# Turning the injection round in an S5 mixer: tokens as the standing operand, states in token order, two modulation panels moved to later joins

## The reference

```python
def s5_scan(u, lam_bar, b_bar, h0, reverse):
    bu = jnp.einsum('bngc,gsc->bngs', u.astype(jnp.complex64), b_bar)
    a = jnp.broadcast_to(lam_bar, bu.shape)
    a_cum, xs = lax.associative_scan(_lin_rec, (a, bu), axis=1, reverse=reverse)
    return xs if h0 is None else xs + a_cum * h0[:, None]
...
        xs_ctx = s5_scan(u_ctx, lam_bar, b_bar, None, reverse)
        h0 = xs_ctx[:, 0] if reverse else xs_ctx[:, -1]
        xs_lat = s5_scan(u_lat, lam_bar, b_bar, h0, reverse)
        y_lat = y_lat + jnp.einsum('bngs,gcs->bngc', xs_lat, c_mat).real.reshape(B, L, D)
```

## Time and profile before

| | |
|---|---|
| median of three timed runs | 2246.18 us (2245.98 to 2246.7) |
| the profiled execution: its time, its span | 2244.69 us, 2242.9 us |
| busy in the span: PE, DVE, ACT, POOL | 2102.9, 1164.0, 865.2, 158.9 us |
| mean granted clock of PE | 0.958 of 2.4 GHz |
| the chain that ended last, by engine | PE 88%, DVE 6%, DMA 3%, ACT 2% |

### The profile page before, as it was taken

One profiled execution on the slowest core, in us unless ns is written; L12 is line 12 of the kernel. 1 busy time (PEld: TensorE's weight loads), 2 busy tenths in 40 slices (PEclk: granted clock), 3 DMA queues, 4 the chain that ended last, 5 costly groups with the idle time before them and its releaser, 6 DMA issues.

```text
span 2242.9 us, 31627 instructions
## 1 busy us (share of the span) xinstructions
PE 2102.9 (94%) x13233; PEld 1648.8 (74%) x13233; DVE 1164.0 (52%) x1961; ACT 865.2 (39%) x1416; POOL 158.9 (7%) x225
## 2 busy tenths in 40 slices
PE   4999999999999989988999999997959899898998
PEld 2756566777787767754558888875948799778997
DVE  2322562656566567636154665765571645526454
ACT  2442233443333453220244334245632544525444
POOL 0000110102001100010001200111120000000000
PEclk8999999999999999999999999998579999999999
DMA  6334442545445546531143433444584555314553
GB/s 256 132 116 175 135 148 68 168 154 182 155 153 175 173 154 224 186 134 65 38 151 118 130 118 115 134 134 166 207 336 135 188 188 188 125 57 150 188 178 105
DMA packets 227243, 342.14 MB, mean 153 GB/s; under 512 B 9590, under 2 KB 190625, under 8 KB 224860
## 3 DMA queue, kind: packets, MB, share of 16 engines
q1 hardware_dynamic: 216064, 310.27, 40.4%
q0 software_dynamic: 10320, 29.58, 4.5%
q10 hardware_dynamic: 716, 0.26, 0.0%
HBM read 317.66 MB, written 24.51 MB: 153 GB/s over the span
## 4 chain that ended last, share of the span: by engine, by line
PE 88%; DVE 6%; DMA 3%; ACT 2%; issue 1%; SPq 0%; ACTq 0%; DVEq 0%
PE bank L956 21%; PE bank L957 20%; PE bank L958 20%; PE bank L819 4%; PE bank L397 4%; PE bank L864 2%; PE bank L2473 2%; DMA mod_ring<-mod_w 2%; PE bank L1722 1%; PE bank L1351 1%; PE bank L637 1%; DMA arena<-mod_w 1%; PE bank L2055 1%; PE bank L627 1%; PE bank L1676 1%; PE bank L1933 1%
## 5 line engine op out<-in xcount | busy, mean ns | idle before, releaser
L956 PE MATMUL bank<-h_hi,w_hi 128*128 128x512 f32 (+1 forms) x1480 | 512.4, 346 | 10.9 <-DVE h_lo L725 10.3
L957 PE MATMUL bank<-h_lo,w_hi 128*128 128x512 f32 (+1 forms) x1480 | 504.9, 341 | 0.0
L958 PE MATMUL bank<-h_hi,w_lo 128*128 128x512 f32 (+1 forms) x1480 | 504.8, 341 | 0.0
L917 DVE TENSOR_TENSOR w_lo<-ring,w_hi 128x1024 fp32r<-128x1024 f32 (+1 forms) x282 | 323.9, 1186 | 285.6 <-ACT w_hi L910 285.5
L956 PEld LDWEIGHTS bank<-h_hi,w_hi 128*128 128x128 f32 x1480 | 283.2, 191 | 49.2 <-DVE h_lo L725 12.3
L910 ACT ACTIVATE w_hi<-ring 128x1024 fp32r<-128x1024 f32 (+1 forms) x282 | 274.0, 1019 | 104.7 <-PE bank L958 103.1
L958 PEld LDWEIGHTS bank<-h_hi,w_lo 128*128 128x128 f32 x1480 | 283.1, 191 | 32.2 <-issue 0.2
L957 PEld LDWEIGHTS bank<-h_lo,w_hi 128*128 128x128 f32 x1480 | 283.6, 192 | 29.5 <-issue 0.2
L956 PE MATMUL bank<-g_hi,w_hi 128*128 128x512 f32 (+1 forms) x704 | 241.1, 342 | 0.0
L957 PE MATMUL bank<-g_lo,w_hi 128*128 128x512 f32 (+1 forms) x704 | 236.9, 337 | 0.0
L958 PE MATMUL bank<-g_hi,w_lo 128*128 128x512 f32 (+1 forms) x704 | 236.7, 336 | 0.0
(11 more groups left out here) (328 smaller groups left out, 2974.1 us busy)
## 6 DMA issues: line engine op xcount, KB each, us to landing
ring<-ffn_w SPq DMA_DIRECT2D x120, 1024.0 KB, 5.1
mod_ring<-mod_w SPq DMA_DIRECT2D x88, 1024.0 KB, 6.9
ring<-ffn_w SPq DMA_DIRECT2D x16, 768.0 KB, 4.6
ring<-hy_w_in SPq DMA_DIRECT2D x12, 1024.0 KB, 5.2
arena<-mod_w SPq DMA_DIRECT2D x8, 1024.0 KB, 17.3
s_in_weights<-arena POOLq DMA_DIRECT2D x32, 256.0 KB, 3.2
s_out_weights<-arena POOLq DMA_DIRECT2D x16, 512.0 KB, 3.5
arena<-s_in_weights SPq DMA_DIRECT2D x8, 1024.0 KB, 10.6
```

The costliest lines, as they stand in the source:

```text
L917: last = unit.tensor_tensor(self.lo[:, i % SPLIT, c:c + w], self.w.slot(i)[:, c:c + w], self.hi[:, i % SPLIT, c:c + w].bitcast(F32), ALU.s ...
L956: nc.tensor.matmul(o, w[0], v[0], start=first, stop=False)
L957: nc.tensor.matmul(o, w[0], v[1], start=False, stop=False)
L958: return nc.tensor.matmul(o, w[1], v[0], start=False, stop=last)
```

## The change

1. In the injection `u` stands (128 x 64) and `et` moves (256 columns: real and imaginary): 4 products for each n, two and two in the left and right 64 columns of the array. The result has chunks on partitions. It is copied to SBUF (`rows`, in the weight ring), by DVE for n = 0 to 3 and by ACT for the rest (`move_injected`), and four 128x128 transposes for each n (`turn_states`) bring states back onto partitions, in banks 4 and 5. ACT copies from there into `e`, in two pieces instead of three.
2. `e` is now [group, re/im, 8 blocks, 8 places]: chunks lie in the order of time. So `forward` and `backward` are one copy each of runs of 32. In `inside`, equal places of all blocks are now 8 words apart; `across` steps over the same distances as before (64 words); in `carries` the table of powers is read with a step of 64 words in the innermost dimension, which was a broadcast before.
3. The context is the first and the latents the second half of a row of `h_split`.
4. Two panels of the modulations leave the join ahead of S5 (with their DMAs on SP); all later panels move up by two, and the last two go into the join in the middle of layer 3. So units are complete at other keys. `et` 4 to 7 are loaded ahead of the modulation refill and the Toeplitz weights.
5. POOL's `carries` wait until all states are in `e`; the Toeplitz products run in plain order.

The diff, cut:

```diff
@@ class S5: layout, places of the modulations @@
-                self.e = area(4096, GROUPS, 2, STEP, 2 * CH // BLK)
+                self.e = area(4096, GROUPS, 2, 2 * CH // BLK, BLK)
+                self.rows = self.t0.rearrange("p (a n) -> p a n", a=2)
-                mods.place((self, "turn"), 0)
-                mods.place((self, "states"), 2, p0 + 0.3)
+                mods.place((self, "states"), 2, p0 + 0.4)
@@ sync @@
-                mods.refill(sp, p0 + 0.1)
                 for qt in range(4):
                     self.tokens(sp, 0, qt)
+                for c in range(4, 8):
+                    inject(c)
                 mods.refill(sp, p0 + 0.2)
@@ vector @@
+                for n in range(2):
+                    self.move_injected(dve, V.tensor_copy, n)
                 dve.wait_ge(self.m_loaded, 16)
...
+                for n in range(2, 4):
+                    self.move_injected(dve, V.tensor_copy, n)
...
-                        prev, cur = self.e[:, gs, :, i - 1, :], self.e[:, gs, :, i, :]
+                        prev, cur = self.e[:, gs, :, :, i - 1], self.e[:, gs, :, :, i]
...
-                        dve.wait_ge(self.e_moved, 3 * gs.stop // 4)
+                        dve.wait_ge(self.e_moved, 2 * gs.stop // 4)
                         inside(gs)
-                        if gs.start == 0:
-                            mods.vector(dve, (self, "turn"))
@@ carries @@
-                tq = [self.tab[:, i, 0:nq, gs].rearrange("p q g -> p g q").unsqueeze(3).to_broadcast([P, n, nq, 4]) for i in range(2)]
-                end = [self.e[:, gs, r, nq, 3:7].unsqueeze(2).to_broadcast([P, n, nq, 4]) for r in range(2)]
+                tq = [self.tab[:, i, 0:nq, gs].rearrange("p q g -> p g q").unsqueeze(2).to_broadcast([P, n, 4, nq]) for i in range(2)]
+                end = [self.e[:, gs, r, 3:7, nq].unsqueeze(3).to_broadcast([P, n, 4, nq]) for r in range(2)]
@@ states, forward, backward @@
-                copy(dst[:, :, :, 0], src[:, :, 3:7, BLK - 1]).then_inc(done, 1)
-                copy(dst[:, :, :, 1:BLK], src[:, :, 4:8, 0:BLK - 1]).then_inc(done, 1)
+                copy(dst, src).then_inc(done, 1)
...
-                copy(dst[:, :, ::-1, BLK - 1], src[:, :, 3:7, BLK - 1]).then_inc(done, 1)
-                copy(dst[:, :, ::-1, BLK - 2::-1], src[:, :, 4:8, 0:BLK - 1]).then_inc(done, 1)
+                copy(dst[:, :, ::-1], src).then_inc(done, 1)
@@ new @@
+            def inject(self, pe, n):
...
+                if n >= 2:
+                    pe.wait_ge(self.placed, self.moved(n - 2))
+                for p in range(2):
+                    for z in range(2):
+                        gb = 2 * p + z
+                        last = nc.tensor.matmul(bank[self.INJECT[n % 2]][64 * z:64 * z + 64, 256 * p:256 * p + 256], self.u[:, 4 * n + gb, :],
+                                                self.et[:, c % 4, 4 * (n % 2) + gb].rearrange("p i n -> p (i n)"), start=True, stop=True)
+                last.then_inc(self.e_summed, 1)
+            def move_injected(self, eng, copy, n):
+                eng.wait_ge(self.e_summed, self.injected(n))
+                if n >= 2:
+                    eng.wait_ge(self.e_summed, self.turned(n - 2))
+                copy(self.rows[:, n % 2], bank[self.INJECT[n % 2]][:, :]).then_inc(self.placed, 1)
+            def turn_states(self, pe, n):
+                pe.wait_ge(self.placed, self.moved(n))
+                if n >= 2:
+                    pe.wait_ge(self.e_moved, 2 * (n - 1))
+                dst = bank[self.STATES[n % 2]][:, :].rearrange("p (a z i j) -> p a i z j", a=2, z=2, i=2)
+                for p in range(2):
+                    for i in range(2):
+                        o = 256 * p + P * i
+                        last = nc.tensor.transpose(dst[:, p, i], self.rows[:, n % 2, o:o + P], ident[:, :])
+                last.then_inc(self.e_summed, 1)
@@ scalar @@
+                    if n == 3:
+                        act.wait_ge(self.placed, self.moved(3))
+                    if 3 <= n < self.NB - 1:
+                        self.move_injected(act, copy, n + 1)
+                    act.wait_ge(self.e_summed, self.turned(n))
...
+                    copy(dst[0:STATE], src[0:STATE]).then_inc(self.e_moved, 1)
+                    copy(dst[STATE:P, :, ::-1], src[STATE:P]).then_inc(self.e_moved, 1)
+                mods.scalar(act, (self, "states"))
@@ joins @@
-            if l == 2:
-                mid.place_mods((2, 0))
+            else:
+                mid.place_mods((2,))
...
-                post.place_mods((2, 2), (len(panels) + 0.1, len(panels) + 0.2))
+                post.place_mods((2, 0), (len(panels) + 0.2, None))
             if l == 2:
-                post.place_mods((2, 0))
+                post.place_mods((2,))
```

More of the change, by code:

```diff
@@ L550, in __init__ @@
                 self.rows = n // 4
-                self.first, self.fills = None, False
+                self.first, self.fills = None, 0
                 self.sq = Tally(y_squared, KD)
@@ L568, in place_mods @@
             def place_mods(self, counts=(2, 2), before=None):
-                self.fills = True
+                self.fills = len(counts)
                 for part, n in enumerate(counts):
@@ L700, in scalar @@
                 if self.fills:
-                    for part in range(2):
+                    for part in range(self.fills):
                         mods.scalar(act, (self, part))
@@ new lines, in turned, with moved @@
+            def turned(self, n):
+                return min(2 * n + 3, 2 * self.NB)
+            def moved(self, n):
+                return n + 1 + (16 if n >= 2 else 0)
+            def inject(self, pe, n):
+                c = n // 2
+                if n % 4 == 0:
+                    for e in range(2):
+                        pe.wait_ge(self.u_loaded[e][n // 4 % 2], 16 * 4 * (n // 8 + 1))
+                if n % 2 == 0:
+                    pe.wait_ge(self.w_loaded[c % 4], 16 * (c // 4 + 1))
+                if n >= 2:
[6 more added lines that the diff above has]
+                last.then_inc(self.e_summed, 1)
@@ L2478, in tensor @@
+            def tensor(self, pe):
+                for n in range(self.NB + 1):
+                    if n < self.NB:
+                        self.inject(pe, n)
+                    if n:
+                        self.turn_states(pe, n - 1)
                 pe.wait_ge(self.m_loaded, 16 * (1 + 8))
@@ L2530, in scalar @@
                 self.backward(act, copy, 0, self.s_moved)
-                for key in ("turn", "states", "scan"):
-                    mods.scalar(act, (self, key))
+                mods.scalar(act, (self, "scan"))
                 act.wait_ge(self.step, sum(self.SCAN))
```

70 lines of the change are left out of this document (24 added, 46 removed).

## The result

The changed kernel takes 2233.76 us (median of four runs, 2232.64 to 2235.67) against 2246.08 us for the kernel before: a ratio of 0.9948, 95% interval 0.9931 to 0.9966. A second set of runs gave 2233.23 against 2243.95 us, 0.9953 (0.9941 to 0.9966). So it is faster, by 11 to 12 us, where the prediction said 2244 with a range down to 2236.

The account below looks back on a forecast made before the run. PE bounds S5's injection, then DVE; after the change DVE bounds the whole mixer. Terms 3.8 - 1.9 + 0.6 - 0.4 - 4.5 = -2.4 against 2244.7 give 2242.3, plus 1.5 for the median 2243.8, said as 2244; range 2236 to 2251 us.

Parts of the forecast that it names:

- DVE's end in S5: End of DVE's `carries` of half 1 in S5: 1667.9 us against 1664.1 before, +3.8 us.
- DVE as the bound of the whole mixer: In S5, DVE never waits again after the first states; its work of 66.8 us at unchanged prices sets the end.
- The floor under rival B: End of S5: POOL's `carries` and the last panels end near 1664 us, limiting the gain to 2238 us.
- rival B: In S5's scan, the step costs only 0.3 to 0.6 ns per element and powers read free; 2238 us at best, 27%.
- The first states at 1579.5 us: Start of DVE's scan in S5: 1579.5 us instead of 1587.21, 7.7 us earlier.
- Stride of `inside`, "I take 0.9": DVE's `inside` in S5: the step of 8 words costs 0.9 ns extra per element, 19.4 us in all.
- `carries`: DVE's `carries` of half 1 in S5: powers read with a step of 64 words cost 2.2 us more.
- Behind the scan: After DVE's scan in S5: ACT's dense forward copy gives -1.9 us, a turn and its bias cost +0.6.
- The turn in the join of layer 2's middle, -0.4: Join in the middle of layer 2: a modulation unit's turn is gone, saving 0.4 us.
- FNet: Join ahead of FNet: without the turn, products start inside the join and end near 1969.5 us, not 1974.35; -4.5 us.
- Rival E: Join ahead of FNet: the products do not start in the join, so that gain falls away; 2248.5 us, 10%.
- Middle of layer 3: Middle of layer 3: two added panels, 1.86 us of PE, stay hidden; +1.9 us without that cover.

Follow-up runs that it names:

- Experiment 3: The changed kernel with the modulation panels, the turn and the refills where they were before the change; 2246.42 us, ratio 1.001.
- Experiment 5: The changed kernel with 26 vector instructions of 512 fp32 elements added ahead of `carries` of half 1, output wrong; one run, 2259.73 us.
- experiment 4: The kernel before with only `e` put in the order of time, injection and panels as before; 2254.59 us, ratio 1.0043.
- experiment 6: The changed kernel, but PE waits for the last tile of the join before FNet's first product; 2239.54 us.
- Experiments 2: The kernel before with the modulation panels moved as in the change and `et` 4 to 7 loaded ahead of the modulation refill; 2233.48 us, ratio 0.9953.
- Experiment 9: The changed kernel with `e` in the old order, which the transposes write so that copies into `e` stay dense; 2224.97 us, ratio 0.9914.
- 10: Experiment 9 with ACT's forward copy of half 1 moved ahead of the rows of the four panels; 2219.76 us, ratio 0.9892.
- 11: Experiment 10 with four modulation panels at `states` and two at `scan`, so two come earlier; 2217.57 us, ratio 0.9875.
- experiment 12: The changed kernel with the dense scan of experiment 9 and the modulation panels where they were before the change; 2231.92 us, ratio 0.9938.

## Why the prediction was wrong

In direction it was near (a small gain), in size it was not: -2.4 us forecast against the one trace, -11.2 measured against it. The step that failed is the first term of the sum, DVE's end in S5: +3.8 us forecast, -1.4 measured (113.1 us behind the reciprocal, before 114.5). The mechanism behind it was right, DVE as the bound of the whole mixer; its start and the price of its strides were mis-sized. The floor under rival B, which set the low end of the range, failed as well. Step by step, with times behind the reciprocal at 1549.56 where kernels are compared:

- **What bounds the kernel, and that DVE would be the bound of the whole mixer: right.** No wait of DVE from the first states to the end of `carries`.
- **The first states at 1579.5 us: 2.5 us too late, the first mis-sized term.** Forecast 29.9 us behind the reciprocal, measured 27.5. The step took PE at the lower clock and starting with DVE's copies. PE had begun 3.1 us before DVE came, and ran all batches but the first two at the upper clock, 1.6 to 1.7 us each and not 2.56; its last transposes ended at 1592.65, where the prediction had 1611. Experiment 3 puts a price on it: with the tokens at the old time DVE waits 4.14 us, the scan starts 4.6 later, and it ends 5.1 later.
- **Stride of `inside`, "I take 0.9": too dear, 19.4 against 16.6 us.** Fourteen steps of 16 groups take 2.30 us against 1.71, seven of 32 groups about 3.97 against 2.78. Experiment 5 gives 0.76 ns per element for every form with a step of 8 words, and experiment 4 shows the same step of 16 groups, 2.33 us, with the old injection. The rows that I took (1152 ns for 512 elements) belong to instructions that were slower by a cause that no run here looked at: the same form takes 1.08 us in experiment 5.
- **`carries`: right.** 11.15 us against 8.75, +2.4 where 2.2 was forecast. On POOL the step was free, where I allowed 4 us.
- DVE's end: 118.3 us behind the reciprocal forecast, 113.1 measured. 2.5 and 2.8 from the two points above, less 0.2 for `carries`, make 5.1 of these 5.2. The spread that the prediction gave to this end was mis-added: both low ends and the earlier start make 1578.5 + 66.8 + 12.9 = 1658.2 and not 1661.4, and both high ends with the later start 1672.5 and not 1671.
- **Behind the scan: right.** From DVE's end to the first product of the gated projection it was 14.2 us and is 12.8: -1.4, forecast -1.3. From there to the reciprocal it is 63.1 us in both.
- **The turn in the join of layer 2's middle, -0.4: did not come.** It stood at 1742.38, behind the reciprocal at 1741.43, so it belongs to the FFN of layer 2: 210.51 and 210.42 us before, 210.66 and 210.40 in the changed kernel.
- **FNet: right in mechanism, 0.9 short.** -5.4 us against -4.5, since PE was at the upper clock from 1960 on (granted clock 1.00 from 1960 to 1966). Rival E is refuted, and experiment 6 shows that the start inside the join is the cause.
- **Middle of layer 3: right.** The added panels cost nothing in the stretch.
- **Rival B's floor: wrong.** It said that POOL and the last panels would cap the gain at 2238. POOL's carries were no slower, ACT's copies for half 0 took 3.97 us instead of 7.7, and the last panel ended at 1651.9, 8 us ahead of DVE. The prediction also kept the floor at 1664 for a DVE that is faster, though it says itself that this chain moves with `across` of half 0, which would then be earlier too. The low end of the range hung on that floor.
- **The base.** The sum was made against one trace, whose time was near the median, but whose part ahead of S5 was longer than in all others. 2.8 of the 8.8 us between forecast and trace are that, the luck of one trace and nothing that the prediction could have found. Why the timed runs differ by 2 to 4 us more than the stretches is not settled: the runs of one kernel spread by up to 8 us, and no experiment looked at the part ahead of S5.

Terms: 5.2 (DVE's end) + 0.9 (FNet) + 2.8 (ahead of S5) + 0.1 (FFNs) + 0.1 (behind the scan) - 0.4 (the turn in the middle of layer 2) = 8.7 of the 8.8.

One remark of the prediction is not borne out: it took the shrinking transposes of the input for a rise of the clock. The granted clock is 1.00 from 12.8 to 16.2 us already, and 1.00 again from 16.2 to 23.0, so what shortened them is open. No term hung on it.

The larger point is what the sum did not ask: which part of the change carries it. Experiments 2 and 3 show it. With the old injection and the old layout, the order of DMAs and panels gives as much in the timed runs as the whole change (10.5 of 10.7 us beside the same runs of before; in the traces from S5 on 6.7 of 8.4), and the rest of the change without that order gives nothing. The turned injection frees some 25 us of PE (29.5 us from first to last record, and 55 before) and removes DVE's 8.4 us of idle time, and the layout that came with it costs DVE 19 us, in a kernel where DVE waits for nothing. Experiment 9 keeps the first without the second; with what it uncovers behind it (10 and 11), 28 us are gained against before, 1.25%. So the turned injection is not worthless: experiment 12, with the old places of the panels, is 14.4 us faster than before, since it scans densely. The Trainium skill, "Vector Engine (DVE) Microarchitecture Reference", § 5.2 Measured stream behaviour on trn2, which the prediction weighed, says that any hop between pairs of adjacent words is free, and experiment 5 agrees for a hop of 8 words (0.69 us). In two points the measurement differs: a step of 2 words is free as well, and 8 words take 1.08 us for 512 elements on one, two or three ports, hardly more than the 1.02 of 64 words, where the page gives more for small steps and for more ports. Its own small step, of 24 words, stands in no run here.

## What to carry to other kernels

When an engine becomes the bound from its first input to its last instruction, everything ahead of that input counts in full: look first at what stands in the DMA queues and in program order ahead of it, since moving panels and four weight loads gave here as much as moving them and rewriting the injection too. A layout change moves its price from one engine to another; if a transpose or another pass writes the data anyway, let it write the order that the bound engine reads densely. After each gain read what is next in program order on the helper engine: the copy that stood 7.3 us behind unrelated rows takes 3.8 us itself, and moving it ahead gave 5 us.

## What was not expected of the hardware

- DVE, fp32, 512 elements: a step of 2 words 0.69 us, of 4 words 1.06, of 8 words 1.08, of 64 words 1.02, dense 0.69 (experiment 5); a second and a third strided operand add nothing (1.08), nor does a PSUM partner (1.07).
- POOL reads with a step of 64 words in the time of a broadcast, 2.33 us for 896 elements, while DVE goes from 1.09 to 1.69.
- PE stayed at the lower clock through 55 us in which it was busy all the time with products of 64 columns and weight loads (clock 0.50), and ran at the upper one through products of 256 columns that alternate with transposes (1.00 from 1567 to 1594).
- Transposes that write a permuted order into PSUM, as in experiment 9, took as long as those of the changed kernel that write runs of 64 words, 0.66 us for four in both.
